# A two-layer decoder step: the convolutions' first taps and the channel norm's squares on ScalarE, weight splits up to six units ahead

## The chip, the cores and the metric

The kernel runs on one core of a Trainium2 chip. The metric is the device time in microseconds of one execution; each version is executed several times, and the median counts.

## What is computed

One inference step of two layers for a prompt group (256 tokens) and a sample group (8 sequences of 8 tokens) that share their weights, 320 tokens in all. A layer is a mixing part with three branches and a feed-forward part (dense in layer 0, eight experts of which each token takes two in layer 1):

```python
z = x @ w_in + b_in
z_a, z_b, z_g, q, z_m = split(z, SPLITS)
u = z_a[..., :512] * sigmoid(z_a[..., 512:])
c_a = causal_depthwise_conv(concat([buf_a, u]), w_conv_a, b_conv_a)        # width 31
y_a = silu(layer_norm(c_a, ln_a_g, ln_a_b)) @ w_a_out
c_b = causal_depthwise_conv(concat([buf_b, z_b]), w_conv_b, b_conv_b)      # width 4
h, h_last = rg_lru(c_b, h0, ...)
y_b = (h * gelu(z_g)) @ w_b_out
y_c = cross_attention(q, mem_k, mem_v) @ w_c_out
g = sigmoid(z_m)                                                           # three gates per channel
x = layer_norm(ALPHA * x + (g0 * y_a + g1 * y_b + g2 * y_c) @ w_mix_out)
x = layer_norm(ALPHA * x + ffn(x))
```

## The kernel before

Channels lie on the 128 partitions and tokens along the free axis, so that a projection of the mixing part is, for each 128 output channels, eight products over the input channels with 320 tokens as the moving side. The weights are float32. To keep the precision, each weight unit (128x1024, 512 KB) is **split**: ScalarE rounds it to a high half `wh` (`make_hi`, L583), VectorE subtracts to get the low half `wl` (`make_lo`, L589), and TensorE (PE) forms three products per block: high by high, low by high, high by low (L1781 to L1783). An output block of 128 channels thus takes 24 matrix multiplications, and one split serves one block.

SP streams the weight units into a ring of six places (`SLOTS`). A place is loaded again when the low half of the unit that lay in it is made (or, for a unit that is used as it is, when PE is done with it). The halves have three places (`SPLITS`). Some units are not split: the caches of keys (`ck`) and values (`cv`) of the sample group, which PE reads from the ring directly. They stand in the stream between the units of `zb` and between the gates' units.

Each engine runs a program written out in order. PE's order for the mixing part of a layer is: `za` (8 blocks, GLU input of branch A), `q`, `k`, `v`, then `zb` with the sample group's scores (`ck`), `zg` (8 blocks), the turned probabilities `pt`, the attention output `o`, and then the list `ATTEND`, in which the eight blocks of the third gate (`g20` to `g27` below) stand among the sample group's attention (`ob`, `ot`) and the sums over channels for the norm of branch A (`mean`, `var`):

```python
ATTEND = [("ob", 0), ("g", 2, 0), ("g", 2, 1), ("ot", 0), ("g", 2, 2), ("g", 2, 3), ("ob", 1), ("g", 2, 4),
          ("mean", 0), ("g", 2, 5), ("ot", 1), ("g", 2, 6), ("g", 2, 7), ("var", 0)]
```

Behind it come `yc` (the projection of the attention output, 8 blocks) and `rg` (the gates of the recurrence; block `rg` n takes the bank of `yc` n, which VectorE empties at L1459). The ATTEND tiles take four PSUM banks in turn, in the order of the list. So g24 has the bank of `ot` 0, and can start only when VectorE has read that one in `samples_lo(0)` (L1418).

Where a split stands in ScalarE's and VectorE's programs is set by one rule, `near` (L596): before the work that goes with PE's step s, an engine makes every split that is fewer than `AHEAD` = 2 splits past those PE is done with at s, and whose unit is fewer than 2 * `AHEAD` = 4 units past the units PE is done with. In stretches where every unit is split the first condition alone decides; where raw units stand between, the second does.

VectorE's work beside the splits: GLU, then branch A's convolution, 31 taps over four groups of 128 channels, each tap as one instruction on the 256 prompt tokens and one on the 64 sample tokens. Tap 0 (L1370, L1372) also adds the bias and stands behind each GLU product; it also releases the bank of `za`. Taps 1 to 30 (`tap(k)`, `mac` L1192) are placed one pass (8 instructions) behind each block of `q`, `k`, `v`, `zb` and `zg`; the last five passes stand in a row ahead of the gates. In the gate loop VectorE makes the splits, and does `conv_b` (branch B's convolution, two groups at a time, 4 first taps at L1339 and 12 others) at n = 0, 1, 2 and 6, `samples_lo(0)` at n = 3, and behind the mean the subtraction and the square (L1432) that `var` sums. ScalarE evacuates blocks with bias and activation (L957 sigmoid of `za`, L891 bias of `zb`, L1007 gates), makes the high halves, and takes the square root behind `var` (L1026).

```python
for n in range(KT):
    split_at(l, "g", 2, n)
    if n == 3:
        samples_lo(0)
    if n in (0, 1, 2, 6):
        conv_b({0: 0, 1: 2, 2: 4, 6: 6}[n])
```

The experts of layer 1 are worked off in a loop of eight turns on every engine (large turns first and last, small ones between), about 100 us each, which the engines run as real loops in their program. Each engine's program before the loop is straight. VectorE and ScalarE have 20 and 10 increments of a semaphore that nobody waits for (`dve_placed`, `act_placed`) at their start.

## Time and profile before

| | |
|---|---|
| median of 3 runs | 1924.13 us (1924.04 to 1924.48) |
| profiled execution | 1922.55 us |
| its span, first to last instruction | 1920.8 us |
| mean granted clock of TensorE | 0.977 |
| busy: PE, VectorE, ScalarE, GpSimd | 94%, 76%, 55%, 8% of the span |
| DMA | 447.10 MB, 233 GB/s over the span |

Times in the rows are microseconds from the start of the span. An engine's row gives start, duration, engine, line, operation and the shapes of output and input; in brackets stands how long the engine had been idle before it, and what ended that. A clock of 1.00 is 2.4 GHz, 0.50 is 1.2 GHz. Layer 0 takes the span up to some 590 us, its gate stage lies at 156 to 201 us; the gate stage of layer 1 lies at 766 to 810 us, and the loop over the experts starts at about 1000 us.

### The profile page before, as it was taken

To read this page: it belongs to the slowest core of one execution; us is meant where nothing else is said; L and a number is where in the kernel's file an instruction comes from. 1 tells how busy PE (TensorE), PEld (TensorE's weight loads), DVE (VectorE), ACT (ScalarE), POOL (GpSimd) and SP (SyncE) were. 2 spreads that over 40 slices of the span, in tenths; PEclk is the share of its full clock that TensorE was granted. 3 is DMA by queue.
4 is the path that set the end of the run, shared out by engine and by line. 5 is a ranking of instruction groups with operands and counts; after the bars stand their busy time and mean duration, and the time that the engine had idled before them with its cause. 6 is when DMAs were issued, how large, how long until landed. Compare 5 with 4: busy or idle time off the path is not lost.

```text
span 1920.8 us, 30248 instructions
## 1 busy us (share of the span) xinstructions
PE 1805.2 (94%) x11495; PEld 1564.1 (81%) x11496; DVE 1454.0 (76%) x2067; ACT 1050.4 (55%) x1191; POOL 146.2 (8%) x159
## 2 busy tenths in 40 slices
PE   7998999899999999899979979999999999999993
PEld 7887899799987988799957767878787888888782
DVE  6999686665535999867585667888888888886766
ACT  4453754543424544475354556677777676775553
POOL 2210000000000111000021001020202020100000
PEclk9999999899999999999989999999999999999997
DMA  7564344354443554534437779999999999896763
GB/s 266 201 229 179 119 145 142 110 167 152 154 143 112 194 213 146 208 132 144 132 116 261 266 289 338 360 355 349 355 357 350 366 341 377 330 386 219 278 241 91
DMA packets 119393, 447.10 MB, mean 233 GB/s; under 512 B 11056, under 2 KB 11184, under 8 KB 118784
## 3 DMA queue, kind: packets, MB, share of 16 engines
q1 hardware_dynamic: 112288, 424.45, 60.3%
q0 software_dynamic: 7008, 21.34, 3.5%
q8 instruction: 64, 1.05, 0.2%
q14 instruction: 33, 0.27, 0.0%
HBM read 435.68 MB, written 12.67 MB: 233 GB/s over the span
## 4 chain that ended last, share of the span: by engine, by line
PE 39%; issue 4%; DVE 3%; ACT 2%; DMA 2%; POOLq 0%; DVEq 0%; SPq 0%; POOL 0%; ACTq 0%
PE psum L2053 12%; PE psum L2054 11%; PE psum L2055 11%; PE psum L2077 2%; ACT wph L639 2%; DMA e_ring<-experts 1%; DVE wpl L645 1%; PE psum L2109 1%; PE psum L2118 1%; PE psum L1767 1%; DVE hT L1711 0%; DVE stats L1201 0%; DMA out_acc<-arena,rows_out 0%; DMA x<-out_acc 0%; DVE arena L1704 0%
## 5 line engine op out<-in xcount | busy, mean ns | idle before, releaser
L645 DVE TENSOR_TENSOR wpl<-e_ring,wph 128x2048 fp32r<-128x2048 f32 x269 | 607.1, 2290 | 95.9 <-ACT wph L639 95.0
L639 ACT CAST wph<-e_ring 128x2048 fp32r<-128x2048 f32 x269 | 502.2, 1904 | 138.2 <-DMA e_ring<-experts 69.6
L589 DVE TENSOR_TENSOR wl<-ring,wh 128x1024 fp32r<-128x1024 f32 x234 | 285.1, 1223 | 198.9 <-ACT wh L583 198.2
L1781 PE MATMUL psum<-xTh,wh 128*128 128x320 f32 x1184 | 376.6, 318 | 35.9 <-DVE wl L589 19.8
L1782 PE MATMUL psum<-xTl,wh 128*128 128x320 f32 x1184 | 371.2, 314 | 0.0
L1783 PE MATMUL psum<-xTh,wl 128*128 128x320 f32 x1184 | 370.9, 313 | 0.0
L583 ACT CAST wh<-ring 128x1024 fp32r<-128x1024 f32 x234 | 243.6, 1046 | 157.8 <-PE psum L1802 71.8
L2053 PE MATMUL psum<-wph,xe 128*128 128x512 f32 (+1 forms) x768 | 297.0, 387 | 16.4 <-issue 13.4
L2054 PE MATMUL psum<-wph,xe 128*128 128x512 f32 (+1 forms) x768 | 292.1, 380 | 0.0
L2055 PE MATMUL psum<-wpl,xe 128*128 128x512 f32 (+1 forms) x768 | 290.1, 378 | 0.0
L1781 PEld LDWEIGHTS psum<-xTh,wh 128*128 128x128 f32 x1184 | 227.2, 192 | 48.3 <-DVE wl L589 28.6
L1782 PEld LDWEIGHTS psum<-xTl,wh 128*128 128x128 f32 x1184 | 227.4, 192 | 0.3
L1783 PEld LDWEIGHTS psum<-xTh,wl 128*128 128x128 f32 x1184 | 227.1, 192 | 0.0
L2053 PEld LDWEIGHTS psum<-wph,xe 128*128 128x128 f32 x768 | 145.8, 190 | 48.6 <-issue 16.7
L1192 DVE SCALAR_TENSOR_TENSOR arena<-arena,par 128x256 f32<-128x256 f32 x576 | 179.3, 381 | 1.4
L2055 PEld LDWEIGHTS psum<-wpl,xe 128*128 128x128 f32 x768 | 145.6, 190 | 29.5
L2054 PEld LDWEIGHTS psum<-wph,xe 128*128 128x128 f32 x768 | 146.1, 190 | 26.9
L2053 PE MATMUL psum<-wph,hT 128*128 128x512 f32 x352 | 142.0, 403 | 4.4 <-DVE hT L1711 4.4
L2054 PE MATMUL psum<-wph,hT 128*128 128x512 f32 x352 | 139.8, 397 | 0.0
L2055 PE MATMUL psum<-wpl,hT 128*128 128x512 f32 x352 | 138.7, 394 | 0.0
L2053 PEld LDWEIGHTS psum<-wph,hT 128*128 128x128 f32 x352 | 66.1, 188 | 26.6 <-issue 11.2
L2055 PEld LDWEIGHTS psum<-wpl,hT 128*128 128x128 f32 x352 | 66.1, 188 | 15.8
(323 smaller groups left out, 2272.7 us busy)
## 6 DMA issues: line engine op xcount, KB each, us to landing
e_ring<-experts SPq DMA_DIRECT2D x264, 1024.0 KB, 6.1
ring<-stream SPq DMA_DIRECT2D x274, 512.0 KB, 3.3
lnp<-rows POOLq DMA_DIRECT2D x4, 1024.0 KB, 5.9
x<-x POOLq DMA_DIRECT2D x3, 512.0 KB, 5.5
arena<-x0T SPq DMA_DIRECT2D x2, 640.0 KB, 5.9
o_a<-arena POOLq DMA_DIRECT2D x2, 540.0 KB, 3.9
o_k<-arena POOLq DMA_DIRECT2D x2, 512.0 KB, 6.9
o_v<-arena POOLq DMA_DIRECT2D x2, 512.0 KB, 8.5
```

Source lines behind the costliest of these rows:

```text
L583: act.copy(wh[:, q % SPLITS, :], ring[:, u % SLOTS, :]).then_inc(hi_done, 1)
L589: dve.tensor_tensor(wl[:, q % SPLITS, :], ring[:, u % SLOTS, :], wh[:, q % SPLITS, :].bitcast(F32), ALU.subtract).then_inc(lo_done, 1)
L639: act.copy(wph[:, SLOT_OF[m % NPOS], :], ring_place(m).rearrange("p u c -> p (u c)")).then_inc(hi_e, 1)
L645: dve.tensor_tensor(wpl[:, s, :], ring_place(m).rearrange("p u c -> p (u c)"), wph[:, s, :].bitcast(F32), ALU.subtract).then_inc(lo_e, 1)
L1192: return dve.scalar_tensor_tensor(out=out, in0=in0, scalar=scalar, in1=in1, op0=ALU.mult, op1=ALU.add)
L1781: pe.matmul(out, h[:, k], hi[:, k], start=(k == 0), stop=False)
L1782: pe.matmul(out, h[:, k], lo[:, k], start=False, stop=False)
L1783: ins = pe.matmul(out, low[:, k], hi[:, k], start=False, stop=(k == kt - 1))
L2053: pe.matmul(out, hi, h, start=first, stop=False, skip_group_check=True)
L2054: pe.matmul(out, lo, h, start=False, stop=False, skip_group_check=True)
L2055: return pe.matmul(out, hi, low, start=False, stop=final, skip_group_check=True)
L2077: ins = pe.matmul(psum[CAP_B * g:CAP_B * g + CAP_B, b, 0:P], xe_b[:, k], w[:, P * k:P * k + P], start=(k == 0), stop=(k == KT - 1), skip_g ...
```

## The change

- `near` allows a unit fewer than `SLOTS` = 6 units past those done (it was 4); the limit of 2 splits stays.
- Tap 0 of branch A's convolution (8 instructions per layer) goes to ScalarE, as activations with scale and bias from SBUF, each behind the sigmoid of the next group, the last behind the split for `q`. VectorE releases the bank of `za` with a semaphore increment.
- Tap 0 of branch B's convolution (16 instructions per layer) goes to ScalarE too, each behind the evacuation of the next block of `zb`.
- The square of the centred channels (128x1280, one per layer) goes to ScalarE, behind all eight gates and ahead of `var`'s square root.
- VectorE gets three semaphore increments that nobody waits for in each of 21 steps of the dense feed-forward part. Counted in the built program, VectorE's part before the loop over the experts goes from 1760 to 1773 instructions, ScalarE's from 1037 to 1089. The loop itself is 273 and 249 instructions in both.

PE, GpSimd and SP have the same instructions in the same order as before.

```diff
--- before.py
+++ after.py
@@ -75,6 +75,7 @@
 MEAN_AFTER = 4
 TAIL, HEAD = T, T + NSAMP
 LAST = 3
+DVE_PLACED = 3
 SCORES = [0, 1, 2, 3, 8, 4, 5, 6, 7, 9]
 BRANCHES = [(2, "yc"), (0, "ya"), (1, "yb")]
 SEG_A = K_A - 1 + DSEQ
@@ -515,7 +516,7 @@
         lg_zero, pos_read = sem("lg_zero"), sem("pos_read")
         glu_done = sem("glu_done")
         conv_b_done = sem("conv_b_done")
-        conv_a_tap = sem("conv_a_tap")
+        conv_a_tap, conv_a_first, conv_b_first = sem("conv_a_tap"), sem("conv_a_first"), sem("conv_b_first")
         negmax = sem("negmax")
         probs = sem("probs")
         dev_ready = sem("dev_ready")
@@ -596,7 +597,7 @@
         def near(u, step):
 
             return (plan.split[u] < sum(done <= step for done in split_steps) + AHEAD and
-                    u < sum(done <= step for done in plan.unit_done) + 2 * AHEAD)
+                    u < sum(done <= step for done in plan.unit_done) + SLOTS)
 
         def four_samples(v, q):
 
@@ -945,6 +946,23 @@
                 act.copy(hidden[:, f, TAIL:HEAD], dh[:, f % 2, SEQ:T]).then_inc(dhh_ready, 1)
 
             for l in range(DEPTH):
+                def first_tap_a(j):
+
+                    act.wait_ge(glu_done, 2 * (JA * l + j + 1))
+                    w, b = col(l, "w_conv_a", K_A * j), col(l, "b_conv_a", j)
+                    act.activation(ca[:, j, 0:SEQ], ua[:, j, 0:SEQ], ACT.Identity, scale=w, bias=b)\
+                       .then_inc(conv_a_first, 1)
+                    act.activation(samp(ca[:, j, SEQ:T]), seg_a(j, 0, DSEQ), ACT.Identity, scale=w, bias=b)\
+                       .then_inc(conv_a_first, 1)
+
+                def first_tap_b(j):
+
+                    emptied(act, l, "zb", j)
+                    w, b = col(l, "w_conv_b", K_B * j), col(l, "b_conv_b", j)
+                    act.activation(cb[:, j, 0:SEQ], zb[:, j, 0:SEQ], ACT.Identity, scale=w, bias=b)\
+                       .then_inc(conv_b_first, 1)
+                    act.activation(samp(cb[:, j, SEQ:T]), seg_b(j, 0, DSEQ), ACT.Identity, scale=w, bias=b)\
+                       .then_inc(conv_b_first, 1)
 
                 for n in range(JA):
                     if n == 3:
@@ -956,8 +974,11 @@
                     made(l, "za", 2 * n + 1)
                     frees(act.activation(sg[:, n], bank(l, "za", 2 * n + 1)[:, 0:T], ACT.Sigmoid,
                                          bias=col(l, "b_in", ZA_G + n)), l, "za", 2 * n + 1)
+                    if n:
+                        first_tap_a(n - 1)
 
                 split_for(tile_of(l, "q", 0).done)
+                first_tap_a(JA - 1)
                 act.wait_ge(hist_ready, HIST * l + 1 + JB + 2)
                 for n in range(JC):
                     made(l, "q", n)
@@ -985,8 +1006,11 @@
                     b = col(l, "b_in", ZB + n)
                     ident_bias(zb[:, n, K_B - 1:K_B - 1 + SEQ], bank(l, "zb", n)[:, 0:SEQ], b)
                     frees(ident_bias(seg_b(n, K_B - 1, DSEQ), samp(bank(l, "zb", n)[:, SEQ:T]), b), l, "zb", n)
+                    if n:
+                        first_tap_b(n - 1)
 
                 act.wait_ge(hist_ready, HIST * (l + 1))
+                first_tap_b(JB - 1)
                 for n in range(JB):
                     if n == 0:
                         split_for(tile_of(l, "zg", 0).done)
@@ -1022,6 +1046,8 @@
                     elif key[0] == "g":
                         gates_of(2, key[2], None)
 
+                emptied(act, l, "mean", 0)
+                act.activation(sg[:], ca[:], ACT.Square).then_inc(dev_ready, 1)
                 made(l, "var", 0)
                 frees(act.activation(dev, bank(l, "var", 0)[:, 0:T], ACT.Sqrt, scale=1.0 / D_A,
                                      bias=eps_c[:, 0:1]), l, "var", 0)
@@ -1042,7 +1068,7 @@
                     made(l, "rg", n)
                     frees(act.activation(rr[:, n], bank(l, "rg", n)[:, 0:T], ACT.Sigmoid,
                                          bias=col(l, "b_rg_a", n)), l, "rg", n)
-                act.wait_ge(conv_a_tap, K_A * (l + 1))
+                act.wait_ge(conv_a_tap, (K_A - 1) * (l + 1))
                 act.wait_ge(tails_ready, 2 * (JA + JB) * (l + 1))
                 for n in range(JB):
                     made(l, "rg", JB + n)
@@ -1328,17 +1354,13 @@
             for l in range(DEPTH):
                 def conv_b(j0):
 
-                    for j in (j0, j0 + 1):
-                        emptied(dve, l, "zb", j)
-                    for k in range(K_B):
+                    dve.wait_ge(conv_b_first, 2 * (JB * l + j0 + 2))
+                    for k in range(1, K_B):
                         for j in (j0, j0 + 1):
                             w = col(l, "w_conv_b", K_B * j + k)
                             for out, in_ in ((cb[:, j, 0:SEQ], zb[:, j, k:k + SEQ]),
                                              (samp(cb[:, j, SEQ:T]), seg_b(j, k, DSEQ))):
-                                if k == 0:
-                                    ins = dve.tensor_scalar(out, in_, w, col(l, "b_conv_b", j), ALU.mult, ALU.add)
-                                else:
-                                    ins = mac(out, in_, w, out)
+                                ins = mac(out, in_, w, out)
                         if k < K_B - 1:
                             link(ins)
                         else:
@@ -1362,20 +1384,18 @@
                     z = bank(l, "za", 2 * j)
                     dve.scalar_tensor_tensor(out=ua[:, j, K_A - 1:K_A - 1 + SEQ], in0=z[:, 0:SEQ], scalar=b,
                                              in1=sg[:, j, 0:SEQ], op0=ALU.add, op1=ALU.mult).then_inc(glu_done, 1)
-                    dve.wait_ge(glu_done, 2 * (JA * l + j) + 1)
                     dve.scalar_tensor_tensor(out=seg_a(j, K_A - 1, DSEQ), in0=samp(z[:, SEQ:T]), scalar=b,
                                              in1=samp(sg[:, j, SEQ:T]), op0=ALU.add, op1=ALU.mult)\
                        .then_inc(glu_done, 1)
                     dve.wait_ge(glu_done, 2 * (JA * l + j + 1))
-                    frees(dve.tensor_scalar(ca[:, j, 0:SEQ], ua[:, j, 0:SEQ], col(l, "w_conv_a", K_A * j),
-                                            col(l, "b_conv_a", j), ALU.mult, ALU.add), l, "za", 2 * j)
-                    ins = dve.tensor_scalar(samp(ca[:, j, SEQ:T]), seg_a(j, 0, DSEQ), col(l, "w_conv_a", K_A * j),
-                                            col(l, "b_conv_a", j), ALU.mult, ALU.add)
-                ins.then_inc(conv_a_tap, 1)
+                    dve.sem_inc(evac[plan.tiles[l, "za", 2 * j].bank], 1)
                 def tap(k):
 
-                    dve.wait_ge(conv_a_tap, K_A * l + k)
+                    if k > 1:
+                        dve.wait_ge(conv_a_tap, (K_A - 1) * l + k - 1)
                     for j in range(JA):
+                        if k == 1:
+                            dve.wait_ge(conv_a_first, 2 * (JA * l + j + 1))
                         w = col(l, "w_conv_a", K_A * j + k)
                         mac(ca[:, j, 0:SEQ], ua[:, j, k:k + SEQ], w, ca[:, j, 0:SEQ])
                         ins = mac(samp(ca[:, j, SEQ:T]), seg_a(j, k, DSEQ), w, samp(ca[:, j, SEQ:T]))
@@ -1426,10 +1446,8 @@
                         conv_b({0: 0, 1: 2, 2: 4, 6: 6}[n])
                     if n == MEAN_AFTER + 1:
                         filled(dve, l, "mean", 0)
-                        dve.wait_ge(conv_a_tap, K_A * (l + 1))
+                        dve.wait_ge(conv_a_tap, (K_A - 1) * (l + 1))
                         frees(mac(ca[:], over(bank(l, "mean", 0)[:, 0:T], JA), -1.0 / D_A, ca[:]), l, "mean", 0)
-                        emptied(dve, l, "mean", 0)
-                        dve.tensor_tensor(sg[:], ca[:], ca[:], ALU.mult).then_inc(dev_ready, 1)
 
                 for n in range(H_C):
                     dve.wait_ge(oh_ready, (H_C + 2) * l + n + 1)
@@ -1567,6 +1585,8 @@
                         emptied(dve, l, "u", f)
                         if f:
                             hidden_lo(f - 1)
+                            for _ in range(DVE_PLACED):
+                                dve.sem_inc(dve_placed, 1)
                     hidden_lo(FT - 1)
                     split_for(last_rows(l, "down", FT))
                     residual(2 * l + 1, l, "down")
@@ -1931,7 +1951,7 @@
                     elif key[0] == "g":
                         blocks((l, *key), xTh, xTl, T)
                     elif key[0] == "mean":
-                        pe.wait_ge(conv_a_tap, K_A * (l + 1))
+                        pe.wait_ge(conv_a_tap, (K_A - 1) * (l + 1))
                         take(pe, l, "mean", 0)
                         for j in range(JA):
                             ins = product(bank(l, "mean", 0)[:, 0:T], ones[:], ca[:, j], j, JA)
```

VectorE at the end of the taps of branch A, ahead of the gates of layer 0 (L1192 taps, L589 splits, L1339 first taps of branch B). Before:

```order
L1192 SCALAR_TENSOR_TENSOR arena<-arena,par 128x256
L1192 SCALAR_TENSOR_TENSOR arena<-arena,par 128x64
L589 TENSOR_TENSOR wl<-ring,wh 128x1024 x3
L1339 TENSOR_SCALAR arena<-arena,par 128x256
L1339 TENSOR_SCALAR arena<-arena,par 128x64
L1339 TENSOR_SCALAR arena<-arena,par 128x256
```

Now (the lines are L1218 and L590), at the same place:

```order
L1218 SCALAR_TENSOR_TENSOR arena<-arena,par 128x256
L1218 SCALAR_TENSOR_TENSOR arena<-arena,par 128x64
L590 TENSOR_TENSOR wl<-ring,wh 128x1024
L1218 SCALAR_TENSOR_TENSOR arena<-arena,par 128x256
L1218 SCALAR_TENSOR_TENSOR arena<-arena,par 128x64
```

Two of the three splits moved ahead into the passes of taps (24 and 32 taps earlier), the third stands alone, and the first taps of branch B are gone behind it.

VectorE around `samples_lo(0)` (L1418 before, L1438 now), layer 0. Before:

```order
L1192 SCALAR_TENSOR_TENSOR arena<-arena,par 128x256
L1192 SCALAR_TENSOR_TENSOR arena<-arena,par 128x64
L1418 TENSOR_TENSOR oTl<-psum,oTh 128x4x32
L589 TENSOR_TENSOR wl<-ring,wh 128x1024 x4
L1192 SCALAR_TENSOR_TENSOR arena<-psum,arena 128x1280
L1432 TENSOR_TENSOR arena<-arena 128x1280
L589 TENSOR_TENSOR wl<-ring,wh 128x1024
```

Now:

```order
L1218 SCALAR_TENSOR_TENSOR arena<-arena,par 128x256
L1218 SCALAR_TENSOR_TENSOR arena<-arena,par 128x64
L590 TENSOR_TENSOR wl<-ring,wh 128x1024
L1438 TENSOR_TENSOR oTl<-psum,oTh 128x4x32
L590 TENSOR_TENSOR wl<-ring,wh 128x1024 x2
L1218 SCALAR_TENSOR_TENSOR arena<-psum,arena 128x1280
L590 TENSOR_TENSOR wl<-ring,wh 128x1024
L1218 SCALAR_TENSOR_TENSOR arena<-arena,par 128x256
```

One split stands directly ahead of `samples_lo(0)` that stood behind it, two fewer stand between it and the subtraction of the mean, and the square is gone.

ScalarE at the end of the gates of layer 0 (L1007, now L1031: gate; L1026, now L1052: square root). Before:

```order
L1007 ACTIVATE arena<-psum,par 128x320
L583 CAST wh<-ring 128x1024
L1007 ACTIVATE arena<-psum,par 128x320
L1026 ACT_TABLE_LOAD
L1026 ACTIVATE arena<-psum,eps_c 128x320
```

Now:

```order
L1031 ACTIVATE arena<-psum,par 128x320
L584 CAST wh<-ring 128x1024
L1031 ACTIVATE arena<-psum,par 128x320
L1050 ACTIVATE arena<-arena 128x1280
L1052 ACT_TABLE_LOAD
L1052 ACTIVATE arena<-psum,eps_c 128x320
```

The square of 128x1280 stands between the last gate and the square root with its table load.

## Rows read from the trace of the kernel before

**Rows 1.** The page's part 1: busy us (share of the span) xinstructions.
```profile
PE 1805.2 (94%) x11495; PEld 1564.1 (81%) x11496; DVE 1454.0 (76%) x2067; ACT 1050.4 (55%) x1191; POOL 146.2 (8%) x159
```

**Rows 2.** Waits of PE, 0 to 1000 us: in total, times, longest us.
```profile
PE psum L1781 <- DVE wl L589: 19.8, 17, 3.5
```

**Rows 3.** Timeline of PE: start us, us, what, [idle before <-releaser]; g20 and g24, both layers.
```profile
161.52 0.64 PE L1781 MATMUL psum<-xTh,wh 128*128 128x320 f32 x1 [3.24 <-DVE wl L589]
...
182.10 0.42 PE L1781 MATMUL psum<-xTh,wh 128*128 128x320 f32 x1 [1.34 <-DVE wl L589]
...
771.44 0.62 PE L1781 MATMUL psum<-xTh,wh 128*128 128x320 f32 x1 [3.49 <-DVE wl L589]
...
791.45 0.41 PE L1781 MATMUL psum<-xTh,wh 128*128 128x320 f32 x1 [1.83 <-DVE wl L589]
```

**Rows 4.** Timeline of VectorE, gate stage of both layers.
```profile
147.91 12.42 DVE L1192 SCALAR_TENSOR_TENSOR arena<-arena,par 128x256 f32<-128x256 f32 x40
160.25 2.35 DVE L589 TENSOR_TENSOR wl<-ring,wh 128x1024 fp32r<-128x1024 f32 x2
...
164.06 1.18 DVE L1339 TENSOR_SCALAR arena<-arena,par 128x256 f32<-128x256 f32 x4
...
180.63 0.29 DVE L1418 TENSOR_TENSOR oTl<-psum,oTh 128x128 fp32r<-128x128 f32 x1
...
190.08 1.49 DVE L1432 TENSOR_TENSOR arena<-arena 128x1280 f32<-128x1280 f32 x1
...
789.97 0.28 DVE L1418 TENSOR_TENSOR oTl<-psum,oTh 128x128 fp32r<-128x128 f32 x1
```

**Rows 5.** Timelines: a first tap on VectorE, a pair of evacuations on ScalarE.
```profile
45.40 0.41 DVE L1370 TENSOR_SCALAR arena<-arena,par 128x256 f32<-128x256 f32 x1
...
89.78 0.68 ACT L891 ACTIVATE arena<-psum,par 128x256 f32<-128x256 f32 x2 [1.90 <-PE psum L1783]
```

**Rows 6.** Waits of VectorE, 100 to 135 us (layer 0) and 708 to 745 (layer 1).
```profile
DVE wl L589 <- ACT wh L583: 3.9, 4, 1.4
...
DVE wl L589 <- ACT wh L583: 4.2, 4, 1.3
```

**Rows 7.** Windows of PE: us, busy (x), clock granted, DMA share, GB/s.
```profile
162.00:170.00 8.00, 8.00 (x40) 0.67 0.89 338
770.00:778.00 8.00, 6.56 (x34) 0.79 1.01 402
178.00:182.00 4.00, 2.76 (x23) 1.00 0.05 13
```

**Rows 8.** Timelines around var and the chain behind it: ScalarE, VectorE, PE.
```profile
199.07 0.53 ACT L1007 ACTIVATE arena<-psum,par 128x320 f32<-128x320 f32 x1 [2.05 <-PE psum L1783]
201.23 0.53 ACT L1026 ACTIVATE arena<-psum,eps_c 128x320 f32<-128x320 f32 x1 [0.33 <-PE psum L1767]
...
258.16 1.27 ACT L1064 ACTIVATE arena<-arena 128x1280 f32<-128x1280 f32 x1
...
202.72 1.23 DVE L589 TENSOR_TENSOR wl<-ring,wh 128x1024 fp32r<-128x1024 f32 x1 [0.54 <-ACT wh L583]
...
216.30 2.87 DVE L1459 TENSOR_TENSOR arena<-psum,arena 128x320 f32<-128x320 f32 x7
...
216.93 3.47 PE L1975 MATMUL psum<-arena,ring 128*128 128x320 f32 x12
```

**Rows 9.** DMA view, 1140 to 1160 us: queue, kind: packets, MB, share of 16 engines.
```profile
q8 instruction: 5, 0.08, 2.3%
q14 instruction: 3, 0.02, 0.3%
```

**Rows 10.** The chain that ended last, around 1150 us: start us, us, what.
```profile
1148.62 4.82 issue
```

**Rows 11.** DMA view, 1160 to 1750 us: all its queues.
```profile
q1 hardware_dynamic: 52755, 203.36, 90.7%
q0 software_dynamic: 2600, 5.33, 3.1%
```


## The prediction

> **What bounds the kernel now.** First the share of each engine: TensorE (PE) is busy for 1805.2 of the 1920.8 us span and VectorE (DVE) for 1454.0 [rows 1]. So only PE's idle time, some 115 us, can be won, and busy time taken from VectorE is worth something only where PE stands waiting for VectorE. The waits of PE over the first 1000 us, the part in which every line of the diff does its work, say how much that is: 19.8 us in 17 waits for the low half of a split (L589), the longest 3.5 [rows 2]. I then read PE's timeline for where these waits are long. Both layers show one pattern: a long wait at the first block of gate columns (g20: 3.24 and 3.49 us), and a shorter one at g24 (1.34 and 1.83) [rows 3]. VectorE's own timeline of that stretch shows why: it works without a break through 40 convolution taps (12.42 us), then splits g20's units, then does the first pair of conv B, and so on to samples_lo(0) at 180.63 and 789.97, and only behind that the split that PE waits for at 182.10 and 791.45 [rows 4]. The place that counts is therefore the end of samples_lo(0).
>
> The profiled run took 1922.55 us, 1.58 below the median 1924.13. The terms below are differences, so I add them to the median. 0.2% is 3.85 us, about what a measurement here can tell from no change.
>
> **1. First taps of conv A to ScalarE.** VectorE loses eight instructions per layer; the wider one of a pair takes 0.41 us [rows 5], so about 0.6 us per column. ScalarE's nearest row, a pair of evacuations of the same widths, takes 0.68 us [rows 5]. The split for q stands on VectorE right behind the last pair, and it needs ScalarE's cast, which now shares ScalarE with a tap of 0.6 us. What VectorE saves it then waits for. From then on the stage is a row of taps on VectorE (about 3.5 us per step), so nothing is gained: +0.1 us per layer, between −0.5 (the pair really saved) and +0.7 (ScalarE's tap wholly in the way). The Trainium skill, "VectorE: DVE Perf Modes", section on the TRN2 errata, gives ScalarE a fixed 224 cycles at 1.2 GHz per instruction from SBUF; by it the pair of 256 and 64 columns would be estimated at 0.64 us, and the sum stays as it is.
>
> **2. Splits up to six units ahead.** This only matters where units that are not split stand in the stream, around the two caches. In the key-cache stage VectorE waits four times for ScalarE's high half, 3.9 us in layer 0 and 4.2 in layer 1 [rows 6]. With the casts allowed earlier, I work out from the order of instructions and these rows that in layer 1 some 2.6 us of waiting is left, so VectorE gets 1.6 us ahead. In layer 0 the cast is held by its weights' own arrival, so I take nothing (0 to 0.4). Both gains only move VectorE's clock; they count at samples_lo(0).
>
> **3. The gate stage.** The splits for g20 and g21 move ahead of the last taps, so the waits of 3.24 and 3.49 us vanish. That alone wins nothing: PE then arrives earlier at g24, which needs the bank that samples_lo(0) empties. So the sum is made on VectorE up to there. It loses three groups of four first taps of conv B (1.18 us busy, next starts 1.22 later [rows 4]): −3.66. In layer 0 it loses two short waits for casts, −0.6. Two further splits now stand ahead of samples_lo(0), +2.3 (two splits are 2.35 us busy [rows 4]). Layer 0: −2.0, its end goes from 180.92 to 178.9. Layer 1: −3.66 + 2.3 − 1.6 = −3.0, from 790.25 to 787.2. Today g24 starts a split later than samples_lo(0) ends (182.10, 791.45). Afterwards that split is already made, and g24 starts at once: 178.9 and 787.3. **Gains: 3.2 and 4.2 us, together 7.3.** The bounds: 2.0 and 3.0 if the split still stands behind; nothing if the wait turns out to be ScalarE's.
>
> **4. What the longer wait does to PE's clock.** PE would end the block before g24 (ob1) (today 182.10 − 1.34 = 180.8 and 789.6 [rows 3]) at 180.8 − 3.24 − 2.6 (the slow clock, below) = 175 in layer 0, and at 789.6 − 3.49 − 1.7 = 784.4 in layer 1, less some 1.6 for the waits of the key-cache stage that go there too. Against 178.9 and 787.3 it idles 4 to 5 us. Today it idles 3.24 us before g20, and over 162 to 170 the mean granted clock is 0.67; in layer 1 3.49 us of idling are followed by 0.79 over 770 to 778 [rows 7]. That is 0.33 · 8 = 2.6 and 0.21 · 8 = 1.7 us lost. Today this is covered, since PE waits for VectorE at g24 anyway. After the change the slow stretch would be g24 to g25, with nothing to wait for, so it costs in full. I take 1.5 per layer, near the smaller of the two rows, since g20 in layer 0 starts with DMA and a cast in arrears besides; ends 0 and 2.7. **+3.0.** The same idle time before g20 is gone, but that gain was covered.
>
> **5. The channel norm's square.** VectorE squares at 190.08, 9 us ahead of var [rows 4]. ScalarE does it now behind all eight gates: gate g27 starts at 199.07 and frees ScalarE 0.43 us later, the square of 128x1280 takes 1.27 us (the same operation stands at 258.16), and the signal to PE costs about 0.2 [rows 8]. Today var starts as g27's block ends, which is when ScalarE's gate starts, 199.07; now 0.43 + 1.27 + 0.2, with a little for the signals on the way about 2.0 later: 201.0. Is that covered? PE has yc to do, but the recurrent gate block rg0 needs the bank of yc0, which VectorE's product at 216.30 empties, and rg0 starts at 216.93 [rows 8]. That product ends a chain that begins at var: the square root at 201.23 (waits for PE), a cast and its split at 202.72 (waits for ScalarE), then reciprocal, norm, sigmoid and products, without a free moment that I can find. From var's end (201.2) to rg0 it is 15.7 us, and it moves with var. So **+4.0** in all, ends 0 (if the chain has slack) and 4.4.
>
> **6. The rest.** 63 semaphore increments in the dense FFN loop of layer 0 lie beside work of VectorE with gaps; no row has one alone, and I take 0 (ends 0 and 1). The turn loop: ScalarE's moves 52 places back in the program, VectorE's 13. Costed at 0; rival D.
>
> Sum: +0.2 − 7.3 + 3.0 + 4.0 = **−0.1 us, so 1924.0.** Without the step on the clock it would be −3.1.
>
> **The rivals.**
> A, the forecast: gain at g24, clock falls, square in the way. 1922.5 to 1926. Chance 0.50.
> B, the clock does not fall, the square is in the way: 1921.0. For it: today's 1.34 us at g24 lies in a window (178 to 182) with a clock of 1.00 [rows 7]. Chance 0.12.
> C, the square is hidden too or nearly: 1924.1 − 7.3 + 0.2 = 1917.0, with the clock falling 1920.0. For it: PE is full with yc until just before rg0, so today's chain may end in time by more than the row shows. Against: 216.30 and one product's 0.41 leave only 0.2 us to 216.93. 0.17.
> D, slower: the turn loop loses its place in ScalarE's instruction memory. Between 1140 and 1160, where the small turns' code is first entered, the instruction queues move five and three packets [rows 9], and the chain has 4.82 us in which PE waits for nothing that shows [rows 10]: 0.6 us per packet. From 1160 to 1750 no instruction packet moves at all, only data [rows 11]. If the 52 places spread ScalarE's loop over one block too many, each of the seven later turns fetches two to four blocks: 7 · 1.2 to 7 · 2.4 = 8 to 17 us, 1932 to 1941. It decides if instruction packets appear in that window. Against: the loop is 249 instructions before and after, and other offsets hold it as well. 0.08. The Trainium skill, "Runtime: NRT & Kernel Launch", section on instruction fetch mechanics, states that a taken branch whose target lies outside the current two-page window forces a fetch; this speaks against moving a loop, and the trace agrees so far as it shows packets at the first entry only.
> E, slower: g24 is held by something else (a cast that waits for its weights), so step 3 gives nothing and the square stays: 1924.1 + 4.0 + 0.2 = 1928.3. 0.08.
> F, slower: ScalarE's casts, now ahead of evacuations, stand waiting for weights and hold PE's banks. Its price is two of the four waits of about 1.3 us [rows 6] per layer, beside E: 1930 to 1934. 0.05.
>
> **How the numbers follow.** Faster by over 0.2% (below 1920.3): C, four tenths of B, a little of A: 0.25. Slower (above 1928.0): D, F, most of E, a little of A: 0.22. The rest, 0.53, within. The range 1917.5 to 1928.5 leaves out D, F, a third of C and a third of E, about 0.2.
>
> **What would show it.** In the changed kernel PE's waits before g20 are gone; those at g24 are 4 to 5 us and name samples_lo (L1438 there); g24 starts about 3 and 4 us earlier relative to the start of its layer; the granted clock dips behind it; var's first product waits about 2 us for L1050; VectorE is busy some 20 us less, ScalarE some 30 us more. The prediction is wrong if the wait at g24 names a split, if the clock stays at 1.00 behind a wait of 4 us, or if rg0 starts as long after g27 as today.

## The result and the profile after

| | before | after |
|---|---|---|
| median | 1924.09 us (1920.58 to 1927.68, 20 runs) | 1926.64 us (1923.66 to 1929.53, 20 runs) |
| profiled execution's span | 1920.8 us | 1927.7 us |
| mean granted clock | 0.977 | 0.973 |

The ratio is 1.0015, with an interval of 1.0009 to 1.0021: slower by 2.5 us, just clear of noise, where 1924.0 was forecast. The time lies in the stated range, and within 0.2% of before, which was held likeliest. But it moved, and the other way from the forecast. Single executions lie up to 3.6 us either side of their median, so the two spans, 6.9 us apart, exaggerate the difference. I read from them where things happen and take sizes from the medians.

The page's part 1 of the changed kernel; it answers to [rows 1]:

```profile
PE 1810.9 (94%) x11495; PEld 1570.2 (81%) x11496; DVE 1436.1 (74%) x2017; ACT 1071.9 (56%) x1241; POOL 133.5 (7%) x159
```

VectorE is 17.9 us less busy, ScalarE 21.5 more, and PE 5.7 more with the same instructions: in this execution it worked longer at the lower clock. The waits of PE from 0 to 1000 us (in total, times, longest), as in [rows 2]:

```profile
PE psum L1801 <- DVE wl L590: 10.4, 14, 2.3
PE psum L1801 <- DVE oTl L1438: 9.0, 2, 4.5
...
PE psum L1787 <- ACT arena L1050: 3.6, 2, 1.8
```

The waits for splits fell from 19.8 to 10.4 us. In their place stand two waits of 4.5 us for samples_lo(0) and two of 1.8 us for the square, as forecast. PE's timeline has them at g24 and var of both layers, with the longest wait for a split at zg3 (the fourth block of `zg`) ahead of them; the row at 188.17 is the mean, which follows g24. [rows 3] are the rows of before:

```profile
132.38 0.41 PE L1801 MATMUL psum<-xTh,wh 128*128 128x320 f32 x1 [2.25 <-DVE wl L590]
...
181.95 0.61 PE L1801 MATMUL psum<-xTh,wh 128*128 128x320 f32 x1 [4.51 <-DVE oTl L1438]
...
188.17 2.32 PE L1787 MATMUL psum<-arena,ones 128*128 128x320 f32 x8
...
203.26 2.42 PE L1787 MATMUL psum<-arena,ones 128*128 128x320 f32 x8 [1.78 <-ACT arena L1050]
...
793.51 0.60 PE L1801 MATMUL psum<-xTh,wh 128*128 128x320 f32 x1 [4.48 <-DVE oTl L1438]
...
814.56 2.42 PE L1787 MATMUL psum<-arena,ones 128*128 128x320 f32 x8 [1.78 <-ACT arena L1050]
```

The first row was not forecast: a wait of 2.25 us at zg3. And g24 of layer 0 starts at 181.95, where 178.9 was forecast and 182.10 was before. The windows of PE (us, busy, clock granted, DMA share, GB/s; as [rows 7]) show what stands behind each of these waits:

```profile
128.00:132.00 4.00, 2.12 (x15) 1.00 0.23 95
132.00:136.00 4.00, 3.62 (x16) 0.64 0.39 133
180.00:184.00 4.00, 2.05 (x8) 0.62 0.89 322
184.00:188.00 4.00, 4.00 (x17) 0.53 1.02 412
792.00:796.00 4.00, 2.48 (x9) 0.50 0.92 350
796.00:800.00 4.00, 4.00 (x18) 0.66 0.97 393
```

In these windows the clock falls three times, twice to its lower level of 1.2 GHz for most of g24's block. Before, it fell behind g20's wait, ahead of another wait that covered it. VectorE and ScalarE in layer 0's gate stage:

```profile
165.57 1.23 DVE L590 TENSOR_TENSOR wl<-ring,wh 128x1024 fp32r<-128x1024 f32 x1 [1.99 <-ACT wh L584]
...
181.52 0.28 DVE L1438 TENSOR_TENSOR oTl<-psum,oTh 128x128 fp32r<-128x128 f32 x1
```

```profile
130.03 1.03 ACT L584 CAST wh<-ring 128x1024 fp32r<-128x1024 f32 x1
...
164.49 1.05 ACT L584 CAST wh<-ring 128x1024 fp32r<-128x1024 f32 x1 [9.70 <-DMA ring<-stream]
...
201.95 1.26 ACT L1050 ACTIVATE arena<-arena 128x1280 f32<-128x1280 f32 x1
```

The third gate unit's cast waits for its weights until 164.49 (161.84 before). PE is 2.5 us later than before by then (the turned probabilities start at 155.26, before at 152.74), and so frees the ring later. VectorE waits 1.99 us for that cast and carries the delay to samples_lo(0). The place of g24 in the whole span mixes all that comes before it. Counted from the first block of `zb` in the same layer (before at 82.47 and 691.43, now at 82.68 and 697.05), g24 starts 0.4 us earlier than before in layer 0 and 3.6 us earlier in layer 1, where 3.2 and 4.2 were forecast.

### The profile page after: what moved, and what is told of

The parts are those of the page before. It is cut to its first block, busy times and chain, and to the rows that moved or that the text cites. A ratio compares the mean times of both kernels' runs of the same rounds, so it can differ in the third digit from the quotient of the medians.

```text
span 1927.7 us, 30313 instructions
## 1 busy us (share of the span) xinstructions
PE 1810.9 (94%) x11495; PEld 1570.2 (81%) x11496; DVE 1436.1 (74%) x2017; ACT 1071.9 (56%) x1241; POOL 133.5 (7%) x159
## 4 chain that ended last, share of the span: by engine, by line
PE 39%; issue 4%; DVE 3%; ACT 2%; DMA 2%; POOLq 0%; DVEq 0%; SPq 0%; POOL 0%; ACTq 0%
PE psum L2073 12%; PE psum L2074 11%; PE psum L2075 11%; PE psum L2097 2%; ACT wph L640 2%; DVE wpl L646 1%; DMA e_ring<-experts 1%; PE psum L2129 1%; PE psum L2138 1%; PE psum L1787 1%; DVE hT L1731 0%; DMA out_acc<-arena,rows_out 0%; DMA x<-out_acc 0%; DVE arena L1724 0%; DVE x L1218 0%
## 5 line engine op out<-in xcount | busy, mean ns | idle before, releaser
L590 DVE TENSOR_TENSOR wl<-ring,wh 128x1024 fp32r<-128x1024 f32 x234 | 286.1, 1224 | 222.9 <-ACT wh L584 221.8
L1218 DVE SCALAR_TENSOR_TENSOR arena<-arena,par 128x256 f32<-128x256 f32 x576 | 179.7, 381 | 0.7
```

Source lines behind the costliest of these rows:

```text
L590: dve.tensor_tensor(wl[:, q % SPLITS, :], ring[:, u % SLOTS, :], wh[:, q % SPLITS, :].bitcast(F32), ALU.subtract).then_inc(lo_done, 1)
L1218: return dve.scalar_tensor_tensor(out=out, in0=in0, scalar=scalar, in1=in1, op0=ALU.mult, op1=ALU.add)
```

## The experiments

The first experiments ask what the square and the place of samples_lo(0) are worth.

**The square back on VectorE** (changed kernel):

```diff
-                emptied(act, l, "mean", 0)
-                act.activation(sg[:], ca[:], ACT.Square).then_inc(dev_ready, 1)
...
+                        emptied(dve, l, "mean", 0)
+                        dve.tensor_tensor(sg[:], ca[:], ca[:], ALU.mult).then_inc(dev_ready, 1)
```

> The changed kernel with one part undone: the channel norm's square is VectorE's again, behind the subtraction of the mean. Theory: the square costs 2.0 us per layer, since the chain behind var moves with it; so var's wait for ScalarE (1.78 us in the changed kernel) goes, and the time falls by about 4.0 us from the changed kernel, to 1922.6, 1.5 below the kernel before. Rival (the chain behind var has slack, and the loss lies in the key-cache stage and the clock): the wait goes but the first recurrent gate block starts no earlier against the last gate block, and the time stays at 1926.6.

Measured: 1922.57 us, ratio to before 0.9991 (0.998 to 1.0002); 4.1 below the changed kernel. The first theory holds; that it does to 0.1 us is luck, with an interval of 2 us either way. The trace says the same: from the mean to rg0 in layer 0 it is 31.2 us in the kernel before and here, and 33.2 in the changed kernel. This run's profile also shows layer 0 without the long wait at zg3. PE's rows at zg3 and g24, and the windows behind the two g24:

```profile
130.22 0.41 PE L1801 MATMUL psum<-xTh,wh 128*128 128x320 f32 x1 [1.19 <-DVE wl L590]
...
178.41 0.60 PE L1801 MATMUL psum<-xTh,wh 128*128 128x320 f32 x1 [4.46 <-DVE oTl L1436]
```

```profile
132.00:136.00 4.00, 4.00 (x29) 1.00 0.52 182
176.00:180.00 4.00, 1.58 (x6) 0.64 1.00 382
180.00:184.00 4.00, 4.00 (x17) 0.51 1.03 414
```

With 1.19 us of waiting at zg3 the clock stays at 1.00 there, and g24 starts at 178.41, which the working had as 178.9. Counted from the first block of `zb`, g24 is 3.6 us earlier than before in layer 0 and 4.6 in layer 1.

Up to zg3 this kernel's program is that of the changed one, so the long wait there is not in every execution. Six of the profiled kernels have the same order of work up to that point. In three of them PE waits 1.9 to 2.3 us at zg3 and the clock falls behind it (0.64, 0.60 and 0.57 over 132 to 136 us); in the other three it waits 1.2 to 1.3 us and the clock stays at 1.00. In all six, and in the kernel before, VectorE waits 1.0 us for the cast behind the exponentials. The rest goes with an earlier cast, which waits for its weights: 1.7 to 2.2 us in the three with the fall, 0.9 to 1.5 in the others. What the fall costs can be read too: from zg3 to the turned probabilities it is 22.9 us with it and 21.5 to 21.6 without. The row and window of another execution with the fall (the changed kernel without its increments, below):

```profile
132.40 0.63 PE L1801 MATMUL psum<-xTh,wh 128*128 128x320 f32 x1 [2.26 <-DVE wl L590]
```

```profile
132.00:136.00 4.00, 3.60 (x14) 0.57 0.40 133
```

**The square alone on ScalarE** (kernel before; the same edit the other way):

> The kernel before with one part of the change alone: the square is ScalarE's, behind all gates. Theory: var starts 2.0 us later in both layers, nothing catches it up: 1928.1. Rival (slack behind var, where PE waits 1.35 us for VectorE anyway and VectorE now has less to do): 1924.1 to 1925.

Measured: 1930.28 us, 1.0035 (1.0022 to 1.0047): 6.0 slower than its own before. The direction holds, and the size is 2 us more than from the other side; its interval, 4.2 to 9.0 us, just takes in the 4.0 of the theory. var's wait is 1.8 us here too. Its profile also has layer 1's g24 waiting 3.84 us with a slow start behind it, where the kernel before waits 1.83 [rows 3]:

```profile
793.27 0.63 PE L1781 MATMUL psum<-xTh,wh 128*128 128x320 f32 x1 [3.84 <-DVE wl L589]
```

The mean follows it 6.1 us later, where it is 3.6 in the kernel before. From the mean to rg0 it is 2.0 us more than before in either layer, so the square itself costs 4.0 here too, and the other 2.4 us of this execution are that slow start. In layer 1 the edit touches nothing ahead of g24. Whether the slow start belongs to this execution alone or to most of this kernel's isn't shown.

**samples_lo(0) one place earlier** (changed kernel):

```diff
-                    if n == 3:
+                    if n == 2:
                         samples_lo(0)
```

> The changed kernel with samples_lo(0) one place earlier in VectorE's gate loop (at n == 2, ahead of the third pair of branch B's convolution). Theory: g24 waits 4.5 us for VectorE's samples_lo(0) in both layers, and the clock falls behind that wait. With samples_lo(0) in front, g24 starts at its split, some 5 us earlier in each layer, its wait is under 1.5 us and the granted clock behind it stays at 1.00, which gives back another 2.4 us per layer: 1911 to 1914. Rival (ScalarE's casts, which wait for weights, hold the gates next): g24 starts earlier, but the following blocks wait instead; 1922 to 1925. Rival on the clock (it falls wherever PE has idled at all here): g24 5 us earlier, clock at 0.6 as before: 1916 to 1918.

Measured: 1912.28 us, 0.9937 (0.9923 to 0.9952): 14.4 below the changed kernel. The waits of PE from 150 to 200 us are these two and no others, and the clock behind g24 (170 to 182 us) is 1.00 throughout. Two waits of 4.5 us and the slow clock behind them (2.6 and 2.4 us, measured below) make 14.0 of the 14.4:

```profile
PE psum L1787 <- ACT arena L1050: 1.8, 1, 1.8
PE psum L1787 <- ACT arena L1025: 1.5, 1, 1.5
```

```profile
174.00:178.00 4.00, 4.00 (x26) 1.00 0.81 296
178.00:182.00 4.00, 4.00 (x26) 1.00 0.98 372
```

**Both edits together:**

> Both edits: samples_lo(0) one place earlier and the square on VectorE. Theory: the two gains are independent: 4 us below the run with samples_lo(0) early alone, 1907 to 1910. Rival (VectorE, which has the square again, becomes the bound between the mean and var): no faster than the run with samples_lo(0) early alone.

Measured: 1906.86 us, 0.9914 (0.9899 to 0.9929), 5.4 below the run before it. The gains add. This beats both kernels.

The next experiments take the clock and the other parts.

**PE kept busy ahead of g24** (changed kernel; adds two unused sums over channels, in the mean's bank):

```diff
                     elif key[0] == "g":
+                        if key[2] == 4:
+                            pe.wait_ge(conv_a_tap, (K_A - 1) * (l + 1))
+                            take(pe, l, "mean", 0)
+                            for _ in range(2):
+                                for j in range(JA):
+                                    product(bank(l, "mean", 0)[:, 0:T], ones[:], ca[:, j], j, JA)
                         blocks((l, *key), xTh, xTl, T)
```

> The changed kernel, in which PE does eight more matrix multiplications of the mean's form (128x320, about 4.6 us in all) in front of g24, where it otherwise waits 4.5 us for samples_lo(0); the bank is the mean's, whose real product overwrites it later. It is an addition that costs PE up to 0.2 us per layer. Theory: behind the wait the granted clock falls to 0.5 to 0.6 for some 6 us, which costs 2.4 us per layer; with PE busy it stays at 1.00, g24 starts where it did and ends 2.4 us earlier: 1926.6 - 4.8 + 0.4 = 1922.2. Rival (the slow blocks behind the wait are slow for another reason, their weights or the banks): 1926.6 to 1927.

Measured: 1922.77 us, 0.9992 (0.9983 to 1.0001): adding 9 us of work that nobody needs made the kernel 3.9 us faster. PE's rows and the windows behind g24 in both layers:

```profile
173.94 4.57 PE L1787 MATMUL psum<-arena,ones 128*128 128x320 f32 x16
178.53 0.39 PE L1801 MATMUL psum<-xTh,wh 128*128 128x320 f32 x1
...
182.12 2.31 PE L1787 MATMUL psum<-arena,ones 128*128 128x320 f32 x8
```

```profile
178.00:182.00 4.00, 3.98 (x26) 1.00 0.99 365
182.00:186.00 4.00, 4.00 (x22) 1.00 0.73 290
786.00:790.00 4.00, 3.97 (x24) 1.00 0.92 356
790.00:794.00 4.00, 4.00 (x23) 1.00 0.90 364
```

From g24's start to the mean it is 3.6 us (178.53 to 182.12). In the changed kernel it is 6.2 (181.95 to 188.17). In layer 1 it is 3.6 against 6.0. So the slow clock costs 2.6 and 2.4 us, not the 1.5 per layer of the prediction. The blocks, their weights and their banks are the same in both kernels, and only the idle time ahead of them is gone, so the slow blocks were a matter of the clock.

**Six units ahead alone** (kernel before):

```diff
-                    u < sum(done <= step for done in plan.unit_done) + 2 * AHEAD)
+                    u < sum(done <= step for done in plan.unit_done) + SLOTS)
```

> The kernel before with splits six units ahead and nothing else. Theory: the wait before g20 goes, but two more splits (2.3 us) stand ahead of samples_lo(0) with all first taps still there, so g24 starts no earlier (layer 0 about 0.5 later, layer 1 about 0.5 earlier); PE idles there 7 us in one piece, and the clock falls behind it, 2.4 us per layer: 1928 to 1930. Rival (the wait before g20 was a cost of its own): 1918 to 1921.

Measured: 1927.04 us, 1.0017 (1.0008 to 1.0026): 3.2 us slower, a little better than expected. The wait before g20 is gone; one of 7 us stands at g24, with the fall of the clock behind it. At zg3 PE waits as long as in the changed kernel's trace, so it is the splits further ahead that gather the small waits there; but here the clock stays at 1.00 behind it:

```profile
130.83 0.41 PE L1781 MATMUL psum<-xTh,wh 128*128 128x320 f32 x1 [2.27 <-DVE wl L589]
...
182.71 0.61 PE L1781 MATMUL psum<-xTh,wh 128*128 128x320 f32 x1 [6.96 <-DVE oTl L1418]
```

```profile
132.00:136.00 4.00, 4.00 (x29) 1.00 0.51 173
182.00:186.00 4.00, 3.29 (x12) 0.50 1.00 340
186.00:190.00 4.00, 4.00 (x18) 0.72 0.29 111
```

**Branch B's first taps alone on ScalarE** (kernel before):

```diff
-                    for j in (j0, j0 + 1):
-                        emptied(dve, l, "zb", j)
-                    for k in range(K_B):
+                    dve.wait_ge(conv_b_first, 2 * (JB * l + j0 + 2))
+                    for k in range(1, K_B):
...
+                    if n:
+                        first_tap_b(n - 1)
```

> The kernel before with branch B's first taps on ScalarE and nothing else. Theory: VectorE reaches samples_lo(0) 3.7 us earlier, so g24 starts when PE comes (its waits of 1.34 and 1.83 us go), the wait before g20 stays: 1924.1 - 3.2 = 1921, a little more where the last two splits catch up. Rival (ScalarE's taps delay its casts in the key-cache stage): a new wait of 1 to 2 us there, 1924 to 1926.

Measured: 1944.70 us, 1.0106 (1.009 to 1.0121), 24 us above the theory and 19 to 21 above the rival. In the gate stages the wait before g20 stays, as forecast, but g24 still waits 0.96 us in layer 0 and 0.95 in layer 1, where none was expected. The loss lies in the loop over the experts, in which no line was changed. The queues from 1160 to 1750 us, and the longest wait of VectorE in that stretch (total, times, longest):

```profile
q1 hardware_dynamic: 50525, 194.82, 88.4%
q0 software_dynamic: 2592, 5.33, 3.0%
q14 instruction: 25, 0.20, 0.1%
```

```profile
DVE arena L1695 <- issue: 42.1, 5, 8.9
```

Against [rows 11] there are 25 instruction packets, five for each turn in the stretch. In the built program the loop had moved from instruction 1760 to 1720, by the 32 first taps and some waits that went with them.

**samples_lo(0) earlier in the kernel before** (the one-line edit of above):

> The kernel before with samples_lo(0) one place earlier and nothing else. Theory: without splits six ahead g24's split stands behind the third pair of the convolution, at the place where PE waits for it today, so moving samples_lo(0) saves only its own 0.3 us per layer: 1923.5. Rival (samples_lo(0) alone held g24): 1914 to 1918.

Measured: 1923.26 us, 0.9998 (0.9989 to 1.0007). In the kernel before, the earlier samples_lo(0) is worth nothing that can be measured, since g24's split is as late. That the 14 us need the splits further ahead is argued, not shown: no run has the earlier samples_lo(0) in the changed kernel with splits four units ahead. In that kernel (below) g24 waits 0.95 us in either layer, and for a split, so little could be won there.

The next experiments settle the placement, and what is left.

**Branch B's first taps alone, VectorE's loop at its place** (42 increments in the dense feed-forward part):

```diff
                             hidden_lo(f - 1)
+                            for _ in range(2):
+                                dve.sem_inc(dve_placed, 1)
```

> The run with branch B's first taps alone on ScalarE took 1944.7 us, 21 more than the kernel before, though its two gate stages ran as the theory has it. In its trace the loop over the experts moves 25 instruction packets from 1160 to 1750 us, where the kernel before moves none, and VectorE stands still five times for up to 8.9 us. This kernel is the same with 42 semaphore increments in VectorE's part ahead of the loop, so that the loop stands at instruction 1762 (before: 1760) instead of 1720; ScalarE's stays at 1071, as in the run of 1944.7. Theory (VectorE's loop lost its place): no instruction packets in the loop, 1921. Rival (ScalarE's loop, 34 places further back, is what is fetched): 1944 again.

Measured: 1918.66 us, 0.9971 (0.9961 to 0.9982): 26 us less than without the increments, and no instruction packet in the loop. ScalarE's loop stands at 1071 in both, so it is VectorE's place that counts. These first taps alone win 5.6 us (3.5 to 7.5 by the interval), 2.3 more than expected. Both waits of layer 0's gate stage got shorter than in [rows 3]:

```profile
161.59 0.41 PE L1790 MATMUL psum<-xTh,wh 128*128 128x320 f32 x1 [2.41 <-DVE wl L589]
...
180.71 0.41 PE L1790 MATMUL psum<-xTh,wh 128*128 128x320 f32 x1 [0.95 <-DVE wl L589]
```

**The changed kernel without its 63 increments** (`DVE_PLACED = 0`):

> The changed kernel without its 63 semaphore increments: VectorE's loop stands at instruction 1710, 63 places ahead. Theory (any place well before 1760 costs fetches each turn, as 1720 did): 1945 to 1950, with instruction packets between 1160 and 1750 us. Rival (only a narrow set of places is bad, and 1710 is out of it): 1926.6, and the increments are for nothing.

Measured: 1926.04 us, 1.0009 (0.9999 to 1.0019), the rival's number. Its loop stands at 1710 and moves no instruction packets; at 1720 it moved 25. The increments gain nothing and cost nothing that can be measured: 1710 would have done.

**Four units ahead again** (changed kernel, the line of `near` as before):

> The changed kernel with splits four units ahead again. Theory: two splits fewer stand ahead of samples_lo(0), so VectorE is there 2.3 us earlier; PE keeps the wait of some 3.3 us before g20 and has none of over 1 us before g24, so no slow stretch is uncovered there. The square's 4 us stay: 1921 + 4 = 1925, about 1.5 below the changed kernel. Rival (splits further ahead are worth their 3 us in the key-cache and gate stages): 1928 to 1930.

Measured: 1925.10 us, 1.0004 (0.9995 to 1.0013), 1.5 below the changed kernel, as the theory had it, though the two intervals overlap.

**Branch A's first taps back on VectorE**, on the fastest kernel so far (loop at 1762):

```diff
-                    dve.sem_inc(evac[plan.tiles[l, "za", 2 * j].bank], 1)
+                    frees(dve.tensor_scalar(ca[:, j, 0:SEQ], ua[:, j, 0:SEQ], col(l, "w_conv_a", K_A * j),
+                                            col(l, "b_conv_a", j), ALU.mult, ALU.add), l, "za", 2 * j)
...
-                    if n:
-                        first_tap_a(n - 1)
```

> The run with samples_lo(0) early and the square on VectorE (1906.86), with branch A's first taps on VectorE again too (VectorE's loop is kept at instruction 1762). Theory: the stage in which these taps stand is VectorE's row of taps and splits either way, and moving them won nothing: 1906 to 1908. Rival (they freed 0.6 us per column that counts): 1909 to 1911. Other rival (ScalarE's taps delayed its cast for q): 1904 to 1905.5.

Measured: 1911.95 us, 0.9933 (0.9919 to 0.9946): 5.1 slower than with them on ScalarE, and 1 us above the rival that gave them a value (1909 to 1911). So these taps do count there, by which route is only partly seen. This execution has the long wait and the fall at zg3, as the one it is compared with has, so the difference isn't there; but in layer 1 PE waits 2.15 us for the probabilities, and the clock falls behind that wait. In the kernel it is compared with, that wait is 1.59 us and the clock over 756 to 764 us is 1.00. Here:

```profile
757.29 3.27 PE L1777 MATMUL psum<-arena 128*128 128x256 f32 x8 [2.15 <-ACT arena L1013]
```

```profile
756.00:760.00 4.00, 2.71 (x8) 0.72 0.02 4
760.00:764.00 4.00, 4.00 (x26) 0.85 0.00 0
```

The last two ask what the cast for zg3 is worth. **One cast moved ahead of five exponentials**, in the changed kernel and in the fastest:

```diff
-                        split_for(tile_of(l, "zg", 0).done)
+                        split_for(tile_of(l, "zg", 1).done)
                         for m in (4, 5, 6, 7, 9):
                             exponentials(m)
```

> The changed kernel with one cast of ScalarE, that for zg3, moved ahead of the five exponentials that stand before the first zg evacuation. It settles what the new wait of 2.25 us at zg3 in layer 0, which the prediction did not have, costs with the slow clock behind it. Theory: VectorE makes the split 1.0 us earlier, PE waits 1.2 us in place of 2.25, and the granted clock behind it stays at 1.00 (it was 0.64 over 132 to 136 us): 1.0 + 1.4 in layer 0, up to 0.7 in layer 1: 1923.5 to 1924.5. Rival (VectorE catches up by itself before the gate stage, so that g24 starts no earlier): 1926 to 1926.6.

> The same edit on the fastest kernel so far (samples_lo(0) early, square on VectorE, 1906.86). Theory: nothing waits between zg3 and rg0 there, so what PE gains at zg3 it keeps: 1904 to 1905. Rival (the rate of branch A's taps on VectorE sets when the probabilities and the gates come): 1906 to 1907.

Measured: 1923.20 us, 0.9994 (0.9985 to 1.0003), 3.4 below the changed kernel, and 1905.23 us, 0.9898 (0.988 to 0.9915), 1.6 below the fastest so far, which is not clear of noise. In the first, zg3 starts at 130.85 (it was 132.38), and the clock stays up:

```profile
130.85 0.41 PE L1801 MATMUL psum<-xTh,wh 128*128 128x320 f32 x1 [0.90 <-DVE wl L590]
```

```profile
132.00:136.00 4.00, 4.00 (x29) 1.00 0.49 153
```

The 3.4 us can't all be read from this trace. Three kernels without the edit kept the clock at 1.00 here too, and this execution took 1925.84, 2.6 above its own median. The cast stood behind the exponentials in the kernel before as well, and the edit was not tried there. So the 3.4 us are what this order of work can give, and not what the change cost.

## Why the prediction was wrong

**The direction.** The sum was −0.1 and the result +2.5. The mechanisms it named are all there. A sum of −0.1 out of terms of −7.3, +3.0 and +4.0 had no direction to stand on: an error of a fifth of a microsecond in any of them turns it. The step that failed is the clock's fall behind g24 (part 4), which was too small by 2.0 us and by itself turns −0.1 into +1.9. The 0.6 us that are left are within noise. Two terms that were nearly nothing in the sum (items 2 and 5) were found to be worth something as well, probably with opposite signs, so that the sum comes so near with this one step mended is partly luck.

1. **The clock behind g24 (part 4) was too small.** I took 1.5 per layer and called it near the smaller of two rows; it lies below both of them (1.7 and 2.6). With PE kept busy, g24 to the mean takes 3.6 us instead of 6.2 and 6.0: 2.6 us in layer 0 and 2.4 in layer 1, near the larger row and my upper bound. Nearest in kind was layer 0's fall before g20, at 0.67 over 8 us [rows 7], since it too ran its whole first block slow. The run with PE busy gained 3.9 net of what it adds.
2. **The key-cache stage (part 2) was taken as nothing in layer 0 ("0 to 0.4"), and that failed in part.** The small waits of that stage, 1.25 and 0.87 us in the kernel before, are gathered into one at zg3 by the splits further ahead. The cast for zg3 stands behind five exponentials and a table load on ScalarE (130.03), and PE arrives there before VectorE has its split. In three of six profiled executions that wait was 1.9 to 2.3 us and the clock fell behind it, which costs 1.3 to 1.4 us beside the longer wait; in the other three it did neither. How much of the median's +2.5 lies here stays open.
3. **g24's start (part 3) was right.** 178.9 was worked out; 178.41 is measured with the square back and 179.15 with the cast ahead, both without the long wait at zg3. Counted from the first block of `zb`, these two are 3.6 and 3.0 us earlier than before in layer 0 and 4.6 in layer 1 (3.2 and 4.2 were forecast). In the profiled changed kernel it is 181.95, which is item 2 passed on through the ring of weights.
4. **The square (part 5) was right.** +4.0 forecast, 4.1 by undoing it; 5.4 and 6.0 in the two other comparisons. From the mean to rg0 the traces have 2.0 us more in each layer.
5. **Branch A's first taps (part 1)** were costed at +0.2 in all with −0.5 to +0.7 per layer. Taking them back costs 5.1 us in the fastest kernel, far outside those ends. On ScalarE a pair takes more than was thought: 0.60 and 0.43 us busy and some 0.8 us until the next instruction, against 0.68 in the nearest row and the estimate of 0.64. What the taps are worth in the changed kernel itself was not tried. A gain of that sort would offset what item 2 costs; that is argued, not shown.
6. **The rest (part 6) was right:** the increments cost nothing that can be measured (0.6 us). Rival D named the wrong engine: ScalarE's loop moved 52 places with no effect, while 40 places on VectorE cost 26 us. That is 1.0 us for each of the 25 packets, where rival D had 0.6. The rule of the Trainium skill, "Runtime: NRT & Kernel Launch", section on instruction fetch mechanics, that a taken branch out of the loaded window forces a fetch, agrees with the 25 packets. It did not tell which places are bad.

Rivals A to F: A's picture (g24 earlier, clock down, square in the way) is what happened, and the time is 0.6 us above A's upper edge. B and C are refuted: the clock fell, and the square was not hidden. D is refuted for this change: from 1160 to 1750 us the changed kernel moves no packet on q14 (one on q8). E was that a cast holds g24 so that nothing is gained there. In layer 0 of the executions with the fall at zg3 it is near the truth: a cast that waits for its weights until 164.49 delays samples_lo(0), and g24 gains 0.4 us. Elsewhere g24 starts as early as forecast. F has no row for it: from 85 to 200 us the only wait of PE that names ScalarE is that for the probabilities, 1.30 us as before. Of the signs, VectorE's 17.9 us less fit the "some 20", ScalarE's 21.5 more fall short of the "some 30".

**Where the gain went.** Alone, branch B's taps are worth −5.6 us, the splits further ahead +3.2, the square +4 to +6. Together that is +1.6 to +3.6, where +2.5 was measured. The change gave back more than this good part won. But in the changed kernel an earlier samples_lo(0) is worth 14 us. In the kernel before it was worth 0.6, which is within noise.

## What to carry to other kernels

When a wait is moved rather than removed, work out where it gathers, and charge the clock's fall behind it in full there: here waits of about 1 us passed without a fall, those of about 2 us went either way (1.3 us more where it fell), and those of 4.5 us cost another 2.4 or 2.6. Look for the instruction that empties the bank and put it ahead of work that nobody waits for; one moved line was worth 14 us in the changed kernel, more than any part of the change. And when instructions are taken out ahead of a real loop, look for instruction packets inside the loop before reading any other number.

## What the hardware showed that I had not expected

- Useless work can pay: 9 us of extra matrix multiplications in PE's idle time made the kernel 3.9 us faster (1926.64 to 1922.77).
- A fall of the clock behind a wait is not sure: at zg3 a wait of 2.25 us was followed by 0.64, one of 2.27 us by 1.00 (splits six ahead alone) and one of 1.94 us by 0.60 (samples_lo(0) early, square on VectorE). With branch B's taps alone, 2.41 us at g20 was followed by 0.63 in layer 0 and 2.60 us by 1.00 in layer 1:

```profile
162.00:166.00 4.00, 4.00 (x21) 0.63 1.01 391
768.00:772.00 4.00, 3.26 (x22) 1.00 0.98 392
```

- The place of a loop is a narrow thing: VectorE's loop of 273 instructions ran without a packet on q14 at 1710, 1760, 1762, 1773 and 1775, and with five packets a turn at 1720. VectorE then stands still for up to 8.9 us a turn.
